# Closing each round in the next round's first slots, spreading new values by GpSimd, and a later page schedule, in a MoBA + mLSTM decoder step

## What is computed

```
xn = rms_norm(x); split(xn @ w_in) -> aq ak av az | mq mk mv mo mz | ga gm | mi mf
attention: q, k = rope(rms_norm(q)), rope(rms_norm(k))
  prompt: causal softmax(q k^T) v             (256 tokens are one block)
  sample: gate = q . mean(k of a block of 256); keep the 3 best of 4 cached blocks,
          softmax over them and the new token, times v (pages fetched through page_table)
mLSTM, per head: w = exp(log decay - m); s = (q k^T) * w; num = s v + w_inter * (q C)
  h = num / max(|den|, exp(-m));  C_new = a_prev * C + sum a_s k v^T ;  n_new likewise
merge: h = rms_norm(h * sigmoid(mo)); y_att = (attn * silu(az)) @ w_proj_attn
       y_ml = (h * silu(mz)) @ w_proj_mlstm
       y = x + (sigmoid(ga) * y_att + sigmoid(gm) * y_ml) @ w_out
```

## Time and profile before

| | us |
|---|---|
| device time, median of 3 runs | 469.66 (469.01 to 469.67) |
| span of the profiled execution, first to last instruction | 467.2 |
| PE busy in it | 456.2 (98%) |
| DVE busy | 394.1 (84%) |
| ACT busy | 294.4 (63%) |
| POOL busy | 100.9 (22%) |
| TensorE clock granted | 1.000, all along |

### The profile page before, as it was taken

How to read it: one execution, slowest core, us unless ns; L and a number is a source line. 1 busy time by engine, 2 the same in 40 slices (tenths; PEclk the granted TensorE clock), 3 DMA queues, 4 the chain that set the end, 5 groups by cost and what they waited for, 6 DMA issues and landing times.

```text
span 467.2 us, 11345 instructions
## 1 busy us (share of the span) xinstructions
PE 456.2 (98%) x3855; PEld 413.8 (89%) x3855; DVE 394.1 (84%) x1610; ACT 294.4 (63%) x490; POOL 100.9 (22%) x181
## 2 busy tenths in 40 slices
PE   6999999999999999999999999999999999999997
PEld 4899899897879888888899889899898898899997
DVE  3898899699999799999899999799999774668861
ACT  4966545686984496995486695666948357324430
POOL 2040421013323213423321332321223110000000
PEclk9999999999999999999999999999999999999999
DMA  8899699749999999999999999998999985457511
GB/s 304 322 353 407 183 322 371 240 158 340 317 416 408 404 368 354 412 410 408 408 380 315 409 412 409 411 372 303 382 415 409 410 334 188 149 180 261 182 48 48
DMA packets 44858, 150.91 MB, mean 323 GB/s; under 512 B 6192, under 2 KB 7796, under 8 KB 44672
## 3 DMA queue, kind: packets, MB, share of 16 engines
q1 hardware_dynamic: 20368, 70.77, 40.8%
q0 software_dynamic: 19008, 67.20, 37.3%
q10 hardware_dynamic: 5424, 12.21, 6.8%
HBM read 137.37 MB, written 12.76 MB: 321 GB/s over the span
## 4 chain that ended last, share of the span: by engine, by line
PE 70%; ACT 10%; DVE 10%; DMA 4%; issue 4%; ACTq 1%; POOLq 0%; SPq 0%; POOL 0%; DVEq 0%
PE pj L534 28%; PE pj L537 13%; PE wk L534 6%; PE pa L717 4%; PE wk L537 3%; DMA kpages<-in_cache_k 3%; DVE kpages L1170 3%; DVE wlo L1071 2%; ACT L838 2%; ACT whi L818 2%; PE wk L487 2%; DVE cslot L1252 2%; PE wk L639 2%; PE wk L673 1%; DMA cst<-in_consts 1%
## 5 line engine op out<-in xcount | busy, mean ns | idle before, releaser
L534 PE MATMUL pj<-xn,whi 128*128 128x264 f32 x1328 | 180.8, 288 | 1.6 <-ACT mqT L976 1.3
L534 PEld LDWEIGHTS pj<-xn,whi 128*128 128x128 f32 x1328 | 168.4, 189 | 10.2 <-issue 6.2
L1071 DVE TENSOR_TENSOR wlo<-wraw,whi 128x1024 fp32r<-128x1024 f32 x112 | 136.1, 1220 | 8.8 <-ACT whi L818 8.3
L818 ACT ACTIVATE whi<-wraw 128x1024 fp32r<-128x1024 f32 x112 | 117.9, 1053 | 23.1 <-PE wk L537 12.9
L1170 DVE CUSTOM_DVE_ANT_0 kpages<-kpages,qbc 128x128 f32<-128x128 f32 x512 | 115.5, 292 | 5.3 <-DMA kpages<-in_cache_k 5.1
L537 PE MATMUL pj<-xn,wlo 128*128 128x264 f32 x664 | 93.8, 284 | 0.4 <-DVE wlo L1071 0.4
L537 PEld LDWEIGHTS pj<-xn,wlo 128*128 128x128 f32 x664 | 85.5, 188 | 0.6 <-DVE wlo L1071 0.6
L404 POOL DMA_DIRECT2D kpages<-in_cache_k x64 | 34.3, 536 | 165.9 <-DVE sco L1170 141.9
L404 POOL DMA_DIRECT2D vpages<-in_cache_v x64 | 33.9, 530 | 57.9 <-issue 38.9
L1170 DVE DVE_READ_ACCUMULATOR2_ANT sco<- 128x1 f32 x512 | 42.8, 84 | 0.0
L717 PE MATMUL pa<-vpages,prob 128*32 128x256 f32 x512 | 34.2, 385 | 1.7 <-ACT prob L876 1.7
(11 more groups left out here) (271 smaller groups left out, 615.0 us busy)
## 6 DMA issues: line engine op xcount, KB each, us to landing
wraw<-in_weights SPq DMA_DIRECT2D x112, 512.0 KB, 6.8
kpages<-in_cache_k POOLq DMA_DIRECT2D x64, 512.0 KB, 8.1
vpages<-in_cache_v POOLq DMA_DIRECT2D x64, 512.0 KB, 10.8
cslot<-in_states SPq DMA_DIRECT2D x16, 512.0 KB, 9.4
out_C_s<-cslot ACTq DMA_DIRECT2D x16, 512.0 KB, 8.1
xres<-in_tokens SPq DMA_DIRECT2D x1, 1056.0 KB, 5.5
out_k_p<-kT ACTq DMA_DIRECT2D x4, 256.0 KB, 10.2
out_v_p<-v_nat ACTq DMA_DIRECT2D x4, 256.0 KB, 4.7
```

Source lines behind the costliest of these rows:

```text
L534: mm(bank[:, 0:T], whi[:, q, k, :], src[:, g, k, :], start=(k == 0 and g == 0), stop=False)
L818: A(whi[:, n % WSPLIT], wraw[:, n % WRAW], ACT.Copy).then_inc(whi_ready, 1)
L1071: V.tensor_tensor(wlo[:, n % WRAW], wraw[:, n % WRAW], whi[:, n % WSPLIT], ALU.subtract).then_inc(wlo_ready, 1)
```

## The change

A `closing(j, i)` is added on PE, ACT and DVE, and takes a round's ending into slots 0 to 5 of the next round (of the tail for the last one): Sigmoid (i = 0), both Silus (i = 1) followed by an explicit load of the table set that holds Ln and Exp together, square and copy of C (i = 2), the norm's Ln and Exp (i = 4) on ACT; P times V and the new C (i = 1), the norm's sums (i = 3) on PE; `hmo` (i = 1), attention times gate (i = 2), the norm's product (i = 5) on DVE. To leave the banks free, both key heads' `norm_sums` now use wk[0] and wk[1], so head 1's waits for head 0's rope. The rows of v are made by 16 small matmuls at i = 8 (a value column as stationary, the identity moving), one ACT copy (`mvq`) and four POOL broadcasts of 512 columns per round into `mvb` (SBUF), which `new_states` reads instead of a PSUM bank. Decay rows stay in SBUF (`stage`) instead of DRAM. Page starts move from 2 + 9b to `STARTS`, value pages are taken in two visits of four, and value loads get slots of their own.

```diff
-START, PERIOD = 2, 9
-SUMS, SELECT, SHIFT, EXP, VALUES, TOTAL, GATHER = 9, 10, 11, 12, 13, 14, 20
+STARTS = [2, 11, 21, 31, 40, 50, 60, 69]
+LAGS = [(9, 10, 11, 12, 14, 20)] * (NB - 1) + [(8, 9, 10, 10, 11, 14)]
+VISITS = [(13, 17)] * (NB - 2) + [(13, 14), (11, 13)]
+VISIT = PAGES // 2
...
+            def spread_values(j, c):
+
+                pool.wait_ge(mv_ready, 2 * j + 2)
+                if c >= 2:
+                    pool.wait_ge(c_ready, NB * j + 2 * (c - 1))
+                elif j:
+                    pool.wait_ge(c_ready, NB * (j - 1) + 2 * (c + 3))
+                nc.gpsimd.partition_broadcast(mvb[:, c % 2, 0:2 * MHD], mvq[c * VC:c * VC + 1, :]).then_inc(v_spread, 1)
+                pool.wait_ge(v_spread, VG * j + c + 1)
...
+                if g < BODY and g % CHUNKS == 10:
+                    spread_values(g // CHUNKS, 0)
+                    spread_values(g // CHUNKS, 1)
+                if g < BODY and g % CHUNKS in (12, 13):
+                    spread_values(g // CHUNKS, g % CHUNKS - 10)
...
                     if n == 0:
-                        pe.wait_ge(c_ready, NB * j - 2) if j else pe.wait_ge(q_ready, HEADS)
-                        pe.wait_ge(attg_ready, 2 * j)
+                        pe.wait_ge(pT_ready, 2 * j) if j else pe.wait_ge(q_ready, HEADS)
+                        pe.wait_ge(h_ready, j)
                     else:
-                        pe.wait_ge(c_ready, NB * j) if j else pe.wait_ge(qs_ready, 2)
-                        pe.wait_ge(mrs_ready, j + 1)
-                    norm_sums(wk[2 * n], wk[2 * n + 1], n, kT[:, n, :])
+                        pe.wait_ge(rs_ready, HEADS + 2 * j + 1)
+                        pe.wait_ge(kT_ready, 2 * j + 1)
+                    norm_sums(wk[0], wk[1], n, kT[:, n, :])
...
+                    for pick in range(2):
+                        for n in range(2):
+                            c = pick * MHD + n * P
+                            for q in range(VG):
+                                col = SEQ + 2 * q + pick
+                                last = mm(wk[3][q * VC:(q + 1) * VC, c:c + P], rawT[:, n, col:col + 1].broadcast_to([P, VC]), ident,
+                                          start=True, stop=True)
...
+            def closing(j, i):
+
+                if i == 0:
+                    act.wait_ge(evac, HEADS + j * CHUNKS + 12)
+                    A(zraw[:, 2], zraw[:, 2], ACT.Sigmoid).then_inc(sig_ready, 1)
+                if i == 1:
+                    act.wait_ge(evac, HEADS + (j + 1) * CHUNKS)
+                    for gate in range(2):
+                        A(zraw[:, gate], zraw[:, gate], ACT.Silu).then_inc(sig_ready, 1)
+                    if j + 1 < JOBS:
+                        nc.scalar.preload_act_table_set("natural_log_exp_and_others")
...
                     dve.wait_ge(fade_ready, NB * j + b + 1)
-                    dve.wait_ge(vbc_ps, 4 * j + b // 2 + 1)
-                    row = (wk[0], wk[3], wk[0], wk[2])[b // 2][:, b % 2 * MHD:(b % 2 + 1) * MHD]
+                    dve.wait_ge(v_spread, VG * j + b // 2 + 1)
+                    row = mvb[:, b // 2 % 2, b % 2 * MHD:(b % 2 + 1) * MHD]
```

More of the change, by code:

```diff
@@ L618, in states_side @@
                 if i == 7:
+                    pe.wait_ge(mrs_ready, j + 1)
                     for n in range(2):
@@ L640, in states_side @@
                                    start=(half == 0 and d == 0), stop=(half == 1 and d == EC - 1))
-                    mm(wk[1][:, MHD:MHD + 2 * NB], ones, qsum[:, :, :], start=True, stop=True).then_inc(qc_ps, 1)
-                if i == 9:
-                    pe.wait_ge(sw_ready, j + 1)
-                    for n in range(2):
-                        last = tr(wk[3][0:NB, n * P:(n + 1) * P], rawT[:, n, SEQ:T], P)
-                    last.then_inc(mvtr_ps, 1)
+                    pe.wait_ge(w_ready, j + 1)
                     part = MHD // VG
@@ L929, in _ @@
                 if i == 10:
+                    act.wait_ge(mvtr_ps, 2 * j + 2)
+                    act.wait_ge(v_spread, VG * j)
+                    A(mvq[:, :], wk[3][:, :], ACT.Copy).then_inc(mv_ready, 1)
                     act.wait_ge(mv_ready, 2 * j + 1)
@@ L1323, in round_end @@
                 new_states(j, (6, 7))
-            def round_close(j):
-                dve.wait_ge(sig_ready, 3 * j + 3)
-                dve.wait_ge(mrs_ready, j + 2)
-                dve.wait_ge(hmo_ready, j + 1)
-                for e in range(EC):
-                    ch.step(V.scalar_tensor_tensor(out=hT[:, e, :], in0=hT[:, e, :], scalar=mhw[:, e:e + 1], in1=mrs[:, :],
-                                                   op0=ALU.mult, op1=ALU.mult))
-                ch.join()
-                V.tensor_tensor(mlg[:, 2 * j:2 * j + 2, :], hT[:, :, :], zraw[:, 1], ALU.mult).then_inc(mlg_ready, 1)
             for g in range(BODY):
@@ L1346, in _ @@
                     split_lo(HEADS + g + LOW)
-                if i == 1 and j:
-                    round_close(j - 1)
                 keys_side(j, i)
```

306 lines of the change are left out of this document (146 added, 160 removed).

## The result

| | before | after |
|---|---|---|
| device time, median | 469.4 us | 483.42 us (480.85 to 485.23) |
| ratio | | 1.030, 95% interval 1.026 to 1.034 |
| span of the profiled execution | 467.2 us | 479.2 us |
| granted clock of TensorE, four runs | 1.00 in the profiled one, 0.999 or 1.00 in those beside the experiments | 0.993, 0.986, 0.982, 0.982 |

The change makes the kernel 14 us slower; 469.8 us was predicted, and 476 was the upper end of the range. The profiled execution is the shortest of the four, and 12.0 us of the loss are in its span. The other runs have no trace; the longer ones have the lower mean clock.

What follows compares the result with a forecast made beforehand. PE, busy 98% of the span, was taken as the bound, DVE next. Terms -1.6 - 4.2 - 5.6 + 11.5 = +0.1 on the 467.2 us span gave 467.3; with the median 2.5 above, 469.8 us, range 463 to 476.

Steps and rivals of the forecast that it cites:

- Rows of v: Making v's rows by 16 small matmuls takes PE 1.1 us a round; net -0.4 a round, -1.6 us in all.
- A visit: 32 value-page visits of 16 records become 16 of 32, each 2.12 us on PE; 38.1 us become 33.9, -4.2.
- Old waits: PE's waits at the rounds' edges, some on ACT, all go: -5.6 us, the most this term can be.
- New wait at i = 3: Head 1's norm sums wait on PE for head 0's rope on DVE: round 1 stall 6.6 us, partly on `wlo`.
- X: End of PE's denominators (93.24 us for round 1), from which the forecast counts when PE and DVE arrive.
- round 2: Same place a round later: DVE needs 34.0 us, PE 32.9, so PE stalls 1.1 us.
- the tail's `wlo`: PE's new waits at the same places in the tail: 0.2 and 1.6 us, together 1.8.
- Round 3: Rope in time, but `wlo` late by 0.6 and 1.4 us in slots 47 and 49: 2.0 us.
- Broadcasts: POOL's 16 broadcasts take 0.8 us each; two in round 1's DVE chain hold it 0.3 each, 0.6 together.
- The second rival: DVE is held at every broadcast, in slots 10 to 16 of each round: 7.4 us, 477 us; chance 0.22.
- Later pages "at nothing": Four key pages (6.8 us of DVE) move into the tail, where DVE has room, at no cost; otherwise up to 3.
- a page load in the tail: Sign against the forecast: PE waiting on a page load in the tail would make the prediction wrong.

## Why the prediction was wrong

It said 467.3 us for the span, and 479.2 was measured. By its own steps:

- **Rows of v: right.** L688 takes 0.99 us a round (84.40 to 85.39), 1.1 was estimated.
- **A visit: right as work of PE, wrong as time.** 1.86 us and little around it, 2.12 was estimated. But the step took 4.2 us of PE's queue for 4.2 us of time. Alone it cost 4.9 us; with later value loads and the decay rows in SBUF it was worth nothing (ratio 1.000).
- **Old waits: right that they go.** No wait of PE on ACT is left; what that brought can't be read off by itself.
- **New wait at i = 3: right.** 6.55 us for 6.6 (that close by luck: both sides came 0.9 us later than reckoned), slot 20 at X + 42.3 for 41.4, the rope's end at X + 38.3 for 37.4, the wait at the sums 1.9 for "some 2"; round 2 0.9 us for 1.1; the tail's `wlo` 1.6 for 1.8.
- **Round 3: size off.** 2.0 us were estimated for slots 46 to 49, the rows have 3.7, and from start to start the four projections take 4.8 us more than 4 x 2.93 (250.64 to 267.17).
- **Broadcasts: the step that was mis-sized.** 0.8 us is the median, but two took 2.2 and 2.5 us. A key page beside one was held 0.45 to 0.48 us, not 0.3, and the step left out the holds elsewhere. All 16 cost 5.2 us by the run without them; the step had 0.6, in round 1's chain alone. The second rival had the mechanism right (held to the end, at most places), and named slots 10 to 16; it priced all broadcasts together, decay rows too, at 7.4.
- **Later pages "at nothing": the step that failed.** It counted DVE's time between slots 64 and 76 (45 us against 48 of PE) and neither the DMA queues nor who needs which page when. In its place the runs showed 8.4 us at slot 74, where PE waits for value pages 54 and 55 behind full queues, and 8.3 us less when the same pages are asked for in the order in which they are needed. The room in DVE wasn't there either (it was busy 35.8 of the 36 us from 340 to 376), though PE didn't wait for it in that stretch. The visits of samples 6 and 7, which the change's table pulls together, were named nowhere in the sum, although "a page load in the tail" stood among what would make it wrong.
- **The clock: missing.** All waits were priced at their length. A fall behind one costs 1.6 us more. One is in the profiled execution (within the 8.4); the other runs, at clocks of 0.986 and 0.982, are 1.7 to 4.4 us longer, which more falls would explain but no trace shows.
- **The shape of the sum.** It put savings and waits into one row of figures. The runs show that the parts do not add: endings, rows of v, gate tables and decay rows in SBUF together change the time by +6.7 or -9.1 us, depending on where key pages, visits and loads stand, and the decay rows alone by -1.2 or -7.4.

What was not tried: norm sums of head 1 in banks of their own, since the other two work banks hold the results of the moved endings there (P times V, then the new C and the mLSTM norm's sums).

## What to carry over

Where two engines are each busy over 90% of a round and coupled by a buffer of two slots, as here, don't count a microsecond off one as a microsecond of time: 6 us less work of PE brought none. Look, slot by slot, at what the other must do there, and move its optional work out of the slots from which you take work. Before a load or its use is moved, write down what all queues carry in that stretch and compare it with the best rate that the trace shows; and read small DMAs that stand behind large ones as late as those. Beside a wait of the matmul engine set what a fall of the clock would take behind it, here 1.6 us, as a risk and not as a certainty. And when a kernel takes one part of a change alone, list every part that it leaves out: in three comparisons here the decay rows through DRAM came along.

## What the runs showed of the hardware beyond that

- A fall of TensorE's clock behind a hold cost 1.57, 1.60 and 1.60 us, whether PE had been held 2.3, 3.6 or 5.0 us.
- 1 KB from DRAM landed 12 us after its issue, behind 512 KB pages on the same engine's queue.
- 14 key-page operations of DVE in the changed kernel were held to the end of the broadcast beside them, by 0.2 to 1.0 us each; the state updates, with two SBUF inputs as well, by 0.4 at most.
